# Two small gain buffers declared behind the masks, in a two-layer hybrid attention trunk

## What is computed

```python
for l in range(2):
    x = x + 0.5 * swiglu(rmsnorm(x, ffn1_norm[l]), ffn1_w_gate[l], ffn1_w_up[l], ffn1_w_down[l])   # D_FF = 2816
    h = rmsnorm(x, mix_norm[l])
    c_q, c_kv, k_pe, q_s, k_s, v_s = split(h @ w_in[l])
    out_a = dense_causal_attention(...)            # 4 latent heads of 128 + 64, from c_q, c_kv, k_pe
    out_b = sliding_window_sink_attention(...)     # 8 query heads of 64, 2 key heads
    x = x + concat(rmsnorm(out_a, ...), rmsnorm(out_b, ...)) @ w_o[l]
    x = x + 0.5 * swiglu(rmsnorm(x, ffn2_norm[l]), ffn2_w_gate[l], ffn2_w_up[l], ffn2_w_down[l])
```

## Time and profile before

| | |
|---|---|
| median of 3 runs | 1009.09 us |
| lowest and highest run | 1000.56 and 1010.95 us |
| span of the profiled execution | 999.5 us |
| mean granted TensorE clock in it | 0.997 |
| TensorE matmuls busy | 966.5 us, 4504 instructions |
| VectorE, ScalarE, GpSimd busy | 565.5, 473.6, 53.0 us |
| transfers | 168.6 MB, 169 GB/s over the span |

### The profile page before, as it was taken

One profiled execution on the slowest core, in us unless ns is written; L12 is line 12 of the kernel. 1 busy time (PEld: TensorE's weight loads), 2 busy tenths in 40 slices (PEclk: granted clock), 3 DMA queues, 4 the chain that ended last, 5 costly groups with the idle time before them and its releaser, 6 DMA issues.

```text
span 999.5 us, 13783 instructions
## 1 busy us (share of the span) xinstructions
PE 966.5 (97%) x4504; PEld 773.4 (77%) x4504; DVE 565.5 (57%) x763; ACT 473.6 (47%) x831; POOL 53.0 (5%) x85
## 2 busy tenths in 40 slices
PE   5999999999899999999989999999998999999998
PEld 4888878888677878788768788887876777878876
DVE  4654545486766644545465454545877665454544
ACT  5543434464656544444355343435456654443433
POOL 2000000022110000000010000000220100000000
PEclk9999999999999999999989999999999999999999
DMA  8765554560044764646357555463501466464641
GB/s 296 248 198 181 174 203 155 182 212 21 22 158 142 232 226 132 227 146 212 124 184 230 192 170 208 153 222 129 190 1 59 156 206 230 138 222 147 208 170 43
DMA packets 46251, 168.61 MB, mean 169 GB/s; under 512 B 5216, under 2 KB 5216, under 8 KB 46208
## 3 DMA queue, kind: packets, MB, share of 16 engines
q1 hardware_dynamic: 44496, 162.02, 48.1%
q0 software_dynamic: 1568, 5.52, 1.8%
q10 hardware_dynamic: 144, 0.52, 0.1%
HBM read 167.00 MB, written 1.05 MB: 168 GB/s over the span
## 4 chain that ended last, share of the span: by engine, by line
issue 75%; PE 17%; POOL 5%; DMA 1%; DVE 1%; ACT 0%; POOLq 0%; DVEq 0%; ACTq 0%; SPq 0%
PE UV L919 3%; PE UV L917 3%; PE UV L918 3%; PE A L917 2%; PE A L918 2%; PE A L919 2%; POOL rs_x L307 1%; DMA raw<-stream 1%; POOL rs_s L307 1%; POOL rs_x L305 1%; POOL rs_m L307 1%; DVE xn L634 1%; POOL gain L285 0%; PE UV L961 0%; ACT whi L367 0%
## 5 line engine op out<-in xcount | busy, mean ns | idle before, releaser
L612 DVE TENSOR_TENSOR wlo<-raw,whi 128x1024 fp32r<-128x1024 f32 x306 | 361.8, 1222 | 113.2 <-ACT whi L367 112.9
L367 ACT ACTIVATE whi<-raw 128x1024 fp32r<-128x1024 f32 x306 | 308.0, 1053 | 114.7 <-DMA raw<-stream 113.8
L917 PE MATMUL UV<-whi,act_hi 128*128 128x512 f32 (+1 forms) x752 | 299.6, 398 | 4.1 <-issue 3.4
L919 PE MATMUL UV<-whi,act_lo 128*128 128x512 f32 (+1 forms) x752 | 292.2, 389 | 0.0
L918 PE MATMUL UV<-wlo,act_hi 128*128 128x512 f32 (+1 forms) x752 | 290.8, 387 | 0.0
L917 PEld LDWEIGHTS UV<-whi,act_hi 128*128 128x128 f32 x752 | 142.6, 190 | 32.7 <-issue 3.9
L919 PEld LDWEIGHTS UV<-whi,act_lo 128*128 128x128 f32 x752 | 142.3, 189 | 30.5
L918 PEld LDWEIGHTS UV<-wlo,act_hi 128*128 128x128 f32 x752 | 142.9, 190 | 27.3
L655 DVE TENSOR_TENSOR ht_lo<-UV,ht_hi 128x256 fp32r<-128x256 f32 x88 | 37.1, 422 | 213.4 <-ACT ht_hi L403 213.4
L403 ACT ACTIVATE ht_hi<-UV 128x256 fp32r<-128x256 f32 x88 | 33.2, 378 | 236.6 <-PE UV L961 236.6
L917 PE MATMUL A<-whi,ht_hi 128*128 128x512 f32 x352 | 141.7, 402 | 0.5 <-DVE ht_lo L655 0.4
(11 more groups left out here) (131 smaller groups left out, 655.3 us busy)
## 6 DMA issues: line engine op xcount, KB each, us to landing
raw<-stream SPq DMA_DIRECT2D x306, 512.0 KB, 4.4
gain<-norm_gains POOLq DMA_DIRECT2D x9, 512.0 KB, 5.7
out<-x SPq DMA_DIRECT2D x2, 512.0 KB, 2.6
sgain<-small_gains POOLq DMA_DIRECT2D x2, 324.0 KB, 5.0
x<-x_in SPq DMA_DIRECT2D x1, 512.0 KB, 3.4
x<-x_in ACTq DMA_DIRECT2D x1, 512.0 KB, 8.2
cs<-rope POOLq DMA_DIRECT2D x1, 128.0 KB, 6.0
cgain<-col_gains POOLq DMA_DIRECT2D x2, 1.0 KB, 5.5
```

What stands on the lines that cost most here:

```text
L367: act.activation(whi_half(unit, half), raw[:, n % RAW, :], ACT.Copy).then_inc(hi_done, 1)
L612: dve.tensor_tensor(wlo_half(unit, half), raw[:, n % RAW, :], whi_half(unit, half).bitcast(F32), ALU.subtract).then_inc(split_done, 1)
L917: pe.matmul(dst, hi, w_hi, start=start, stop=False, skip_group_check=True)
L919: return pe.matmul(dst, lo, w_hi, start=False, stop=stop, skip_group_check=True)
```

## The change

The declarations of sgain and cgain move from before cs to behind masks. Nothing else is edited: the instructions, their order, the waits and the transfers are the same; only addresses differ.

```diff
         gain = sb("gain", [P, 2, D])
-        sgain = sb("sgain", [P, SG])
-        cgain = sb("cgain", [P, 2])
         cs = sb("cs", [P, TB, 2, ROPE])
         xn = sb("xn", [P, D])
         rot = sb("rot", [P, 2 * 640])
...
         ident = sb("ident", [P, P])
         ident_b = sb("ident_b", [P, P], BF16)
         masks = sb("masks", [P, 2, P], BF16)
+        sgain = sb("sgain", [P, SG])
+        cgain = sb("cgain", [P, 2])
         consts = sb("consts", [P, 2, 16])
```

## The result

| | before | after |
|---|---|---|
| median of 20 runs each | 1003.68 us | 998.17 us |
| span of the profiled execution | 999.5 us | 995.6 us |
| mean granted TensorE clock in it | 0.997 | 0.996 |

The ratio is 0.995, 95% interval 0.9928 to 0.9971: a real gain of half a percent, 5 us, against a forecast of 6.2 us. (With 20 runs the median of before is 1003.7; the first three runs had 1009.1.)

A forecast was written before the change was run, and what follows sets the result against it. The prediction took the spacing of TensorE's matmuls as the bound, with the FFN's ht_lo chain close behind. Of 9.7 us saved on ht matmuls 6.2 arrive, other terms nothing: 1009.1 - 6.2 = 1002.9 us, range 992 to 1011.

The forecast's parts named there:

- The spacing: Down matmuls on ht: 12 spacings fall from 2.80 to 2.72 us, 0.11 us per run with the up run behind.
- the two like streams of before: Down products on ht against the mix's input products on act, otherwise equal: 233.3 against 226.7 ns per matmul.
- I take the address as the reason: ht starting 64 bytes past a multiple of 128, act on one, explains the 6.6 ns per matmul.
- the address does nothing: Rival: something else sets ht apart, such as its place in SBUF; no gain, time 1009 us; chance 0.27.
- What arrives: In the FFN, the wait for ht_lo takes back part of the 9.7 us saved on ht matmuls; 6.2 us stay.
- 32 runs of the 88 are lost and 56 stay: In 8 steps of each FFN the ht_lo wait absorbs the saving; 56 x 0.11 = 6.2 us remain.
- the savings behind the transposes: Faster 512-column runs after each pair of h transposes: taken at nothing, bound a gain of 4.4 us.
- The sum: Whole kernel: 6.2 us saved, 993.3 us for the profiled execution and 1002.9 us on the median.
- Transposes and the attention: Moved operands there taken at nothing; transposes might lose 1.8 us, attention products on qt, kt and v gain 2 us.
- The absolute time: Median of the three runs shown, 1009.1 us, less 6.2 us: 1002.9 us.
- All of it arrives: Rival: the ht_lo chain shortens with TensorE, gain 9.7 us, up to 16 with transposes and attention; 993 to 999 us; chance 0.13.
- The new place is worse: Rival: moved ht, work and ident collide with whi's reads, 0.11 us more per run of 12; 1015 us; chance 0.05.

The follow-up runs named there:

- the reordered kernels: Kernel before and changed kernel, each with ht for t = 1 put ahead of the sixth split except in each FFN's last step: ratios to before 0.9965 and 0.9889.
- the second reordering: ht for t = 1 ahead of the sixth split, old order kept in each FFN's last step: 0.9965 on the kernel before, 0.9889 on the changed one.

## Why the prediction was right, and where not

**The spacing.** Right in size and place: 12 down spacings from 2.80 to 2.72 us and the up run behind them from 2.75 to 2.72, by exactly the difference that the two like streams of before had shown. That comparison was the step that carried the forecast.

**Its reason.** "I take the address as the reason" holds, but the address rule it was given, a start at a multiple of 128, is wrong. ht at such starts is slow (only ht moved, ht 128 further), and ht, act and the weights all 64 past one are fast. What counts is that stationary and moving operand have the same start modulo 256. The change brought ht there only because act and the weights already lay so, and 2624 bytes take ht's distance from 64 to 0. The rival *the address does nothing* fell: a pad of 64 or of 128 bytes, with nothing else changed, takes the gain away. By the Trainium skill, SBUF — State Buffer, section Operand start alignment, an operand may start at any multiple of its element size. That is a rule of what is legal, and both layouts meet it; in the runs here they differ by 3% per 512-column matmul.

**What arrives.** The mechanism was right: a wait took back what was saved ahead of it. From ScalarE's copy of ht for t = 0 to the end of ht_lo for t = 1, the chain takes 11.05 us before and 11.08 after, mean of 32, so a faster TensorE does not shorten it; and in the reordered kernels, where it is off the path, all that the 18 runs save arrives. The size was off. The term "32 runs of the 88 are lost and 56 stay" gives 10 x 0.11 = 1.1 us per 18 runs, and 0.62 was measured (0.25 to 0.86 by the choice of kernels). So the wait was to take 0.89 us per FFN, and it took 1.5 to 1.8; in the list of waits it was to stand at 10.7 us, and it stands at 13.7.

One part of the difference has a name. A wait costs more than its length: behind it the down run starts slower. The first spacing of such a run is 0.34 us instead of 0.23 (912.44 to 912.78 in the timeline above). Over its 11 spacings, a down run whose first matmul starts over 260 ns behind the last up matmul takes 0.10 us longer before (12 runs) and 0.15 after (23 runs) than in the reordered kernels. There are more of them in the changed kernel, and they make up 1.2 of the 1.7 us lost within the down runs of all four FFNs before, and 3.3 of 4.0 after. A second part is likely but not shown: the savings behind the transposes, 18 x 0.02 = 0.36 us, were taken at nothing, and may end in the wait as well (the kernel with only work moved needs no more than the others with ht at 0). Whether late transfers add to it is open too; the longest wait, 1.28 us, stands behind a piece of the stream for which ScalarE had waited 1.97 us.

The prediction also let all of the last four down runs of each FFN arrive, 4 x 0.11 us. From the start of the nineteenth down run to the last matmul, the changed kernel saves 0.16 us per FFN, and so does the reordered one; why no more, no run shows.

**The sum.** 6.2 us forecast, 5.0 measured (2.9 to 7.2 by the interval). The traces give less than the medians: the FFNs account for 4 x (0.62 + 0.16) = 3.1 us. The 20 runs of each kernel form two groups (see the clock, below); the 12 in the lower group have medians of 1001.7 us before and 997.6 after, 4.1 us apart. So the agreement with 6.2 owes something to the scatter. Transposes and the attention were rightly taken at nothing, or nearly: transposes of xn, qkn and work start 109 ns apart in both kernels, and the products on qt, kt and v differ by at most 1 ns (medians). On the moved buffers the groups of VectorE and ScalarE change by at most 3 ns.

**The absolute time.** 1002.9 was made on a median of three runs which, by the 20, was 5 us high; the measured median is 998.17. Part of what the prediction called the kernel's scatter has a cause of its own, below.

**The rivals.** *All of it arrives* did not happen here, and it comes near in the reordered kernels, where the FFNs take 172.60 us without the change and 170.08 with it, 10.1 us for four; it needed another edit. *The new place is worse* did not happen, but its mechanism exists: the weights moved by 64 bytes make act's and ht's runs slow alike, at 233 ns.

## What to carry to other kernels

Compare the start-to-start spacing of equal matmuls that differ in one buffer: 3% was readable there, while the recorded weight load was as long as before (188 ns) and the recorded matmul on ht fell by 5 of 395 ns at most. Where weight loads of fp32 alternate with 512-column matmuls, as here, give the stationary and the moving buffers the same start modulo 256 bytes, and assert it beside the declarations, since any small buffer declared between them can shift it. Other types were not tried, and the 192-column products here did not react. And before a gain is booked, find the chain that ends just ahead of it: here more than half of it went into a short wait, and came back only when one work item was put behind another.

## What the runs showed of the hardware

**The distance effect itself.** Four distances between stationary and moving start, modulo 256, read off 512-column fp32 pairs: 0 gives 226.7 ns per matmul, 32, 64 and 128 give 232 to 233.3. The recorded weight load of ht is 188 ns in both. That the two reads get in each other's way is the likely reading, and no run shows it or its cause.

**The runs' scatter comes from the clock.** The kernel with ht 32 bytes further had a span of 1003.8 us, 8 us more than with ht 256 further, though its FFNs were no slower than before's. Windows of TensorE in the mix of the first layer (busy us and count of PE, PEld, DVE, ACT, POOL; granted clock; share and GB/s of DMA), that kernel first, then the changed one:

```profile
245.70:262.80 17.10, 13.86 (x92) 11.11 (x91) 13.81 (x36) 10.40 (x48) 1.83 (x2) 1.00 0.00 1
262.80:280.00 17.20, 17.20 (x52) 10.05 (x52) 8.32 (x19) 6.97 (x18) 0.89 (x2) 0.52 0.09 30
```

```profile
245.70:262.80 17.10, 15.15 (x92) 12.31 (x90) 13.46 (x34) 10.99 (x49) 1.84 (x2) 0.90 0.00 1
262.80:280.00 17.20, 17.20 (x89) 11.03 (x89) 13.26 (x26) 11.99 (x32) 0.89 (x2) 1.00 0.21 64
```

Behind a window of the attention in which TensorE was busy 13.86 of 17.10 us and waited in many small gaps, the clock fell to its lower level, 1.2 GHz, for about 17 us: 52 matmuls in a stretch where 89 ran in the changed kernel, whose own fall was 3.4 us. The kernel before, profiled, had no fall there, with 14.13 us busy in the same window, so the windows don't tell why. The kernel with the moved weights had the same long fall in the mix of the second layer: a clock of 0.50 from 762.7 to 779.8 us, in a span of 1013.6. Among the runs of the kernel before that were timed beside the second reordering, those of 1008 to 1011 us had a mean granted clock of 0.987 to 0.992 and those of 999 to 1005 us one of 0.994 to 1.000. A mean granted clock of 0.988 instead of 0.996 over 1000 us is 8 us, about what one fall of 17 us costs at half the clock (an estimate from these figures). So the 10 us between this kernel's runs, which was taken as its scatter, is likely for the most part one long fall of the clock; the profiles that show it are those of two other kernels.
